# Low splits moved in VectorE's order, and a small fp32 matmul ahead of three units of each FFN

## The reference

```
def hybrid_layer(x, gain, w_in, f_bias, w_branch, w_out):      # first block, twice
    h = rms_norm(x, gain); proj = h @ w_in                     # q, k, v, gates, merge logits
    oa, ob, oc = moba(...), dsa(...), forgetting(...)          # each times silu(gate)
    y = einsum(stack([oa, ob, oc]), w_branch)
    return x + sum(sigmoid(merge_logit) * y) @ w_out
...
x = rms_norm(x, final_gain)
for layer in range(2):                                         # second block
    mod, mod_c = silu(c) @ ada_w[layer] + ada_b[layer], silu(c_ctx) @ ada_w[layer] + ada_b[layer]
    h   = modulate(x,   norm1_g[layer], sh1,  sc1)
    h_c = modulate(ctx, norm1_g[layer], csh1, csc1)
    if layer == 0: y, y_c = even_mixer(h, ...), even_mixer(h_c, ...)     # ends in "@ w_out"
    else:          y = neighbourhood_attention(q, k, v, k_c, v_c, rpb) @ odd_w_o
    x = x + g1 * y
    x = x + g2 * conv_ffn(modulate(x, norm2_g[layer], sh2, sc2), w_up, conv_w, conv_b, w_down)
    if layer == 0: ctx goes the same way as x
return x
```

## Time and profile before

| | us |
|---|---|
| runs, median of three | 1611.9 (1608.91 to 1612.96) |
| the profiled execution | 1592.3 |
| its span, first to last instruction | 1590.5 |
| TensorE busy | 1541.7 |
| VectorE busy | 1039.8 |
| ScalarE busy | 754.3 |
| GpSimd busy | 97.5 |

### The profile page before, as it was taken

The page is one execution under the profiler, slowest core; times in us unless marked ns, Lnnn a source line. Parts: engine busy times, 40 slices in busy tenths (PEclk is TensorE's granted clock), DMA queues, the critical chain, the costliest instruction groups (busy, mean ns, idle before and its releaser), DMA issues.

```text
span 1590.5 us, 31408 instructions
## 1 busy us (share of the span) xinstructions
PE 1541.7 (97%) x13587; PEld 1474.1 (93%) x13587; DVE 1039.8 (65%) x1347; ACT 754.3 (47%) x1132; POOL 97.5 (6%) x79
## 2 busy tenths in 40 slices
PE   6999999999999999999999999999999999989999
PEld 5998999999998999999899999999999996889999
DVE  5878667577877675655457668886445447666675
ACT  5554555455455554554346321333245426655453
POOL 0311000003010000000010000000010102000000
PEclk9999999999999999999999999999999999989999
DMA  8677454566775546522034657754334424255754
GB/s 272 213 239 226 147 182 142 180 222 211 239 238 159 186 148 207 174 80 80 28 107 146 199 178 233 239 186 143 90 116 146 115 80 96 76 148 153 232 170 136
DMA packets 312333, 260.92 MB, mean 164 GB/s; under 512 B 24066, under 2 KB 298498, under 8 KB 312068
## 3 DMA queue, kind: packets, MB, share of 16 engines
q1 hardware_dynamic: 294260, 253.52, 50.2%
q10 hardware_dynamic: 17936, 5.40, 1.6%
HBM read 257.85 MB, written 1.05 MB: 163 GB/s over the span
## 4 chain that ended last, share of the span: by engine, by line
PE 76%; DVE 9%; issue 8%; ACT 6%; DMA 1%; POOL 0%; ACTq 0%; DVEq 0%; SPq 0%; POOLq 0%
PE banks_g L1388 33%; PE banks_g L945 23%; PE banks_g L1118 5%; PE banks_g L935 4%; DVE w_lo L2462 2%; PE banks_g L1260 2%; PE banks_g L968 1%; PE bank_s L1066 1%; ACT w_hi L1761 1%; PE bank_o L1093 1%; PE bank_t L1079 1%; ACT probs L1725 1%; DVE w_lo L2167 1%; ACT w_hi L1565 1%; PE banks_g L927 1%
## 5 line engine op out<-in xcount | busy, mean ns | idle before, releaser
L1388 PE MATMUL banks_g<-h_hi,w_lo 128*128 128x256 f32 x1296 | 360.7, 278 | 3.9 <-DVE w_lo L2462 2.9
L1388 PE MATMUL banks_g<-h_lo,w_hi 128*128 128x256 f32 x1296 | 359.0, 277 | 0.0
L1388 PE MATMUL banks_g<-h_hi,w_hi 128*128 128x256 f32 x1296 | 359.0, 277 | 0.0
L2462 DVE TENSOR_TENSOR w_lo<-raw,w_hi 128x2048 fp32r<-128x2048 f32 (+1 forms) x100 | 207.6, 2076 | 103.3 <-ACT w_hi L1761 103.2
L2167 DVE TENSOR_TENSOR w_lo<-raw,w_hi 128x2048 fp32r<-128x2048 f32 x92 | 212.4, 2311 | 69.4 <-ACT w_hi L1565 68.9
L1388 PEld LDWEIGHTS banks_g<-h_hi,w_lo 128*128 128x128 f32 x1296 | 244.3, 189 | 5.9 <-DVE w_lo L2462 3.3
L1388 PEld LDWEIGHTS banks_g<-h_lo,w_hi 128*128 128x128 f32 x1296 | 244.3, 188 | 0.1
L1388 PEld LDWEIGHTS banks_g<-h_hi,w_hi 128*128 128x128 f32 x1296 | 244.0, 188 | 0.0
L945 PE MATMUL banks_g<-h_hi,w_lo 128*128 128x256 f32 x800 | 225.4, 282 | 0.0
L945 PE MATMUL banks_g<-h_hi,w_hi 128*128 128x256 f32 x800 | 221.8, 277 | 0.0
L945 PE MATMUL banks_g<-h_lo,w_hi 128*128 128x256 f32 x800 | 221.7, 277 | 0.0
(11 more groups left out here) (406 smaller groups left out, 3274.0 us busy)
## 6 DMA issues: line engine op xcount, KB each, us to landing
raw<-w_in SPq DMA_DIRECT2D x76, 1024.0 KB, 5.0
raw<-w_up SPq DMA_DIRECT2D x88, 512.0 KB, 5.1
ada_raw<-ada_w SPq DMA_DIRECT2D x24, 1024.0 KB, 7.0
raw<-w_down SPq DMA_DIRECT2D x32, 704.0 KB, 4.4
raw<-w_branch SPq DMA_DIRECT2D x12, 1024.0 KB, 5.0
ada_raw<-ada_t SPq DMA_DIRECT2D x12, 1024.0 KB, 4.9
late_raw<-ada_t SPq DMA_DIRECT2D x12, 1024.0 KB, 5.0
raw<-qkv SPq DMA_DIRECT2D x12, 1024.0 KB, 4.9
```

Of the source, the lines that this page charges most:

```text
L1388: last = nc.tensor.matmul(to, w[:, c, m0:m0 + P], a[:, c, s_ * SEQ:s_ * SEQ + SEQ], start=(m, s_, c, n) == (0, 0, 0, 0), stop=(m, s_, c, n ...
L2462: nc.vector.tensor_tensor(w_lo[:, u % SLOTS, 0:n], raw[:, u % SLOTS, 0:n], w_hi[:, u % SLOTS, 0:n].bitcast(F32), ALU.subtract).then_inc(dv ...
```

## The change

Five moves in the order of the splits, a new order inside unit eo 0, and six new matmuls.

```diff
@@ layer_order: the context rows' entries 1 to 3, up to three units later @@
-        if 41 <= n <= 44:
-            order.append(("ctx prep", n - 41))
+        order.extend(("ctx prep", m) for m, at in enumerate((41, 44, 44, 45)) if n == at)
@@ end_order, down0 units 14 and 15, before the second block's first unit @@
                 order.append(("ahead", "nq", 0))
+                order.append(("ahead", "nq", 1))
+                chunks("10", 0, 5, KC)
                 part("down0", KC + 6, 1, 6)
-                chunks("10", 0, 5, KC)
-                order.append(("ahead", "nq", 1))
                 part("down0", KC + 7, 1, 7)
@@ end_order, the even mixer's output @@
     for i in range(4):
+        if i == 0:
+            order.append(("ahead", "eo", 2))
         part("eo", i, 0, 2 * i, 2 * i + 1)
-        if i < 2:
-            order.append(("ahead", "eo", i + 2))
+        if i == 1:
+            order.append(("ahead", "eo", 3))
@@ end_order, the attention's output; unit wo 3 no longer splits up1 1 itself @@
         order.append(("unit", "wo", i))
+        if i == 2:
+            order.append(("ahead", "up1", 1))
@@ TensorE, unit eo 0 of the x tokens (of_rows: the three products of chunk c, half m) @@
+                    if (kind, i, j) == ("eo", 0, 0):
+                        for c in (0, 1, 2, 4, 5, 6, 3, 7):
+                            pe.wait_ge(dve_steps, dve_.at(f"a lo{c}" if c < 4 else f"b lo{c - 4}"))
+                            if c == 3:
+                                for c1 in (0, 1, 2, 4, 5, 6):
+                                    of_rows(gb, wh, wl, c1, 1, c1 == 0, False)
+                            of_rows(gb, wh, wl, c, 0, c == 0, False)
+                        for c in (3, 7):
+                            last = of_rows(gb, wh, wl, c, 1, False, c == 7)
@@ TensorE, ahead of the products of units 2, 3 and 4 of each FFN @@
+                            if kind in ("up0", "up1") and j == 0 and 2 <= i <= 4:
+                                nc.tensor.matmul(gb[0:32, 0:HD], ones[:, 0:32], ones[:, 0:HD], start=True, stop=True)
@@ VectorE, end of the first block: both first low splits behind the last output unit @@
-                        if i >= 2:
+                        if layer < DEPTH - 1 and i >= 2:
                             first_low(i - 2)
+                        elif i == 3:
+                            first_low(0)
+                            first_low(1)
```

More of the change, by code:

```diff
@@ L1234, in down_pair, with of_rows @@
                             mm.then_inc(pe_steps, pe_.step(f"job{ks[n]}", f"unit{u0 + n}"))
+            def of_rows(gb, wh, wl, c, m, first, last):
+                for n, (w, a) in enumerate(((wl, f_hi), (wh, f_lo), (wh, f_hi))):
+                    mm = nc.tensor.matmul(gb[:, m * SEQ:m * SEQ + SEQ], w[:, c, m * P:m * P + P], a[:, c, 0:SEQ],
+                                          start=first and m == 0 and n == 0, stop=last and n == 2)
+                return mm
             for what, *arg in END:
@@ L1264, in _ @@
                         continue
+                    if (kind, i, j) == ("eo", 0, 0):
[7 more added lines that the diff above has]
+                            last = of_rows(gb, wh, wl, c, 1, False, c == 7)
+                        last.then_inc(pe_steps, pe_.step(f"job{k}"))
+                        continue
                     for m in range(wide // P):
                         for c in range(kcs):
-                            if (kind, i, j, m) == ("eo", 0, 0, 0):
-                                pe.wait_ge(dve_steps, dve_.at(f"a lo{c}" if c < 4 else f"b lo{c - 4}"))
                             if (kind, i, j) in SUMS_INSIDE and (m, c) == (wide // P - 1, 4):
@@ L1827, in _ @@
                     late = kind == "up0" and i < 2
-                    if u + AHEAD < len(END_UNITS) and not late:
+                    if u + AHEAD < len(END_UNITS) and not late and (kind, i) != ("wo", 3):
                         high(u + AHEAD)
```

## The result

The changed kernel takes 1589.3 us (median of 4 executions, 1586.9 to 1590.4) against 1610.4 us (4 executions, 1605.3 to 1613.0); the ratio is 0.9884, 95% interval 0.9843 to 0.9924. It is faster by 1.2%, and the time lies 3.3 us above the forecast of 1586. Its profiled execution took 1589.1 us, span 1587.3.

A forecast was written before the change was run, and what follows sets the result against it. TensorE was taken as the bound, through matmul spacing and waits. Gains 4.1 + 1.9 + 1.7 + 1.2 less 2.4 for leads make 6.5 us; 1592.3 - 6.5 = 1585.8, taken as 1586, range 1580 to 1592.

The forecast's parts named there:

- A: Both FFNs: leads re-draw the matmul spacing, so slow streams turn fast and fast ones stay; 1586 us, chance 0.50.
- Even mixer's and attention's output projection: Reordered splits shorten TensorE's waits in both output projections: 1.9 us (1.0 to 2.2) and 1.7 us (0 to 3.2).
- Second block's first unit: Queries nq 0 and nq 1: splits placed together remove a TensorE wait and the half clock behind it, 4.1 us.
- End of the first block: Context-row preparation and first low splits moved to shorten two TensorE waits: 1.2 us gained, bounds -1.0 and 3.0.
- The longer chain for the last output unit: End of the first block: chain grows from 7.3 to about 9.7 us, against the 10.9 us of two units.
- Leads: Six small fp32 matmuls before units 2, 3 and 4 of each FFN: 0.4 us each, 2.4 us unhidden cost.
- Sum of the moves: Gains of the moved splits at four places, 4.1, 1.9, 1.7 and 1.2 us, before the leads' cost.
- the base: Three timed runs, 19.6 us above the profiled execution, had both FFNs slow: 4752 matmuls at 4.4 ns, 20.9 us.
- a new draw, not a switch: TensorE's stream: a small fp32 matmul draws the spacing anew, 113.4 or 117.8 ns, rather than switching it.
- Rival B: FFNs: leads do not turn the stream, or the 19.6 us has another cause; only splits count, 1605.4 us, chance 0.34.
- Rival C: Only one FFN is turned, or only one was slow: 1591.5 or 1598.4 us, chance 0.08.
- D: Leads leave the stream slow in FFNs that ran fast: price 20.9 us, 1626 us, chance 0.08.

The follow-up runs named there:

- second trace of before: The kernel before, unmodified, profiled once more in a follow-up run: 1607.6 us.
- set 2: Second batch of follow-up executions, each against the kernel before; the changed kernel, unmodified, ran again in it: 1588.2 us, ratio 0.9897.
- set 3: Third batch of follow-up executions; the changed kernel without the leads of unit 2 took 1588.2 us there, 0.9936 against the kernel before.

## Why the prediction was right, and where not

The forecast (A, 1586 us) and its two halves held: the moved splits take waits off TensorE, and the leads keep the first FFN at the fast spacing. Step by step:

- **Even mixer's and attention's output projection**, forecast 1.9 + 1.7 us: 3.2 us by undoing them. In the stretches of the traces it is 1.9 and 1.9. The wait left at eo 3 is 0.21 us where 0.4 was expected; that for the norm sum is 2.35 in the first trace of the changed kernel and 1.94 in the second, where 1.8 was expected.
- **Second block's first unit**, forecast 4.1 us (2.0 to 4.2): 2.4 us by undoing it, though wait and half clock both went as the text said. In the traces the stretch is 3.9 to 4.2 us shorter in all ten with the new order, so the term was right. That the whole showed only 2.4 us isn't explained; the ranges of the two kernels touch (1590.3 to 1596.0, 1585.0 to 1591.0).
- **End of the first block**, forecast 1.2 us: 1.9 us by undoing it, 2.0 by the stretches. The second wait fell by more than I took: 0.79 us in the first trace of before was the shortest of the four with the old order, the others have 1.53, 2.15 and 2.17. The longer chain for the last output unit, which I had put at nothing, cost 0.69 us at 670.93, in the second trace of the changed kernel 0.28. In the first pair of traces the waits fell by 0.96 and 0.23 us and 0.69 came new, with 10.2 us of half clock in both, and the stretch seemed to gain nothing.
- **Leads**, forecast 0.4 us each: 0.43, so 2.6 us for six where 2.4 were taken.
- **Sum of the moves**, forecast 8.9 us before the leads' cost: 9.5 and 8.6 group against group, 7.5 as the sum of the three undone parts (2.4 + 3.2 + 1.9), 9.9 by the stretches of the traces.

The step that failed is the base: "the three runs had both FFNs at the slow spacing and the profiled one had them at the fast one". The second trace of before shows only the first FFN slow, worth 12.0 us and not 20.9; the second was fast in 13 of 14 traces but for the first few units, and in the one with a single lead in front of unit 2 its last 864 matmuls were slow. The rest of the 19.6 us is the choice of executions: the profiled one lay 3.7 us below the median of its own lower group (1592.3 against 1596.0 over 41 low executions in three sets), and the median of the three runs, 1611.9, lay 3.5 us above that of the upper group (1608.4 over 47). Part of the 3.7 us shows in the traces: the end of the first block ran 1.6 to 3.2 us shorter there than in the three others with its order. That 19.6 came so near to 20.9 was luck. The forecast of 1586 starts from the profiled execution and so from a base that was 3.7 us too low; that is about all that it missed by, and the range of 6 us to each side held it. By the runs the account is 1608.4 (the upper group, in which all four of the first comparison lay) - 12.0 (spacing) - 9.9 (moves, by the stretches; 7.5 by undoing) + 2.6 (leads) = 1589.1, or 1591.5 with 7.5; measured 1589.1.

A second reading did not hold: the prediction calls a small fp32 matmul in the stream "a new draw, not a switch". Behind the wait in front of unit 2 the spacing does differ between two traces of one kernel (fast and slow for the kernel before, slow and fast for the changed one); behind a group of small fp32 matmuls in a running stream it was settled, in each of the four places counted above, by the group and the spacing that came in.

Rival B (leads are pure cost) is refuted by the leads alone, 0.9958 with an interval below 1. The Trainium skill, TensorE: Matmul & The Clock Gate (Back-to-back issue gap), gives one gap for one number of columns. The traces disagree: here the same 2712 matmuls take 307.62 or 319.65 us at full clock. Rival C (one FFN turned) is near the truth as to the size of the slow part. D didn't come: of 76 fp32 leads in a running stream in ten traces, 69 met a fast stream and left it fast, 7 a slow one, of which 6 turned it. Behind the wait in front of unit 2 the stream came out slow in three of eight traces with a lead there, and in three of six without. So the forecast's theory, that fast stays fast and slow is turned by each lead, holds in 75 of 76 cases of a running stream; for the lead behind the wait these traces show no effect.

How much the leads bring depends on how often the first FFN would be slow. For the kernel before that was 4 of 4 executions in the first comparison, then 20 of 29, 14 of 23 and 9 of 32. The ratio of the changed kernel moves with it: 0.9884 in the first comparison, 0.9897 in set 2; in set 3 the kernel with leads in front of units 3 and 4 alone had 0.9936.

Open: what sets the spacing behind a wait; why an fp32 lead keeps a fast stream and an fp32r lead doesn't (two leads of the latter in one trace), where other fp32 groups turn it over; and where all of the 8 us of scatter inside the lower group come from. The traces show parts of it: the first matmul starts up to 2.1 us later in one than in another (the first load), the end of the first block differs by up to 3.2 us between traces of one order, and some short stretches run slow.

## What to carry over

A profile is one execution. Before its time is used as a base, set it against the spread of the timed ones: two groups with nothing between are a state to be found, and count its matmuls per window first. Undo parts one at a time and compare groups with like groups; a pair of spans showed 3.2 us where the moves gave about 9. To price one move, measure its stretch between the same two instructions in every trace at hand: that told 4.0 us from 2.4 where whole times could not. In a TensorE-bound stream of this form a tiny fp32 matmul (0.43 us) can only pay where the stream would run slow and more than some 100 matmuls follow (0.43 us over 4.4 ns, an estimate), and in a running stream rather than behind a wait; two of them did as well as three.

## What was not expected of the hardware

- How long the clock stays at half differs between executions at one place: at the end of the first block the stretches add up to 6.8 us in three of the 14 traces, 10.2 in nine and 13.7 in two. At the output projection they were 10.2 us in all four traces that have its old order, and 6.8 us in six of the ten with the new one.
- One fp32r matmul form has two spacings at full clock, 113.3 and 117.8 ns, and keeps one for up to 2776 matmuls: 12.0 us, or 0.75% of the kernel.
- The spacing can change where the stream is broken. Behind one wait it came out fast in eight traces and slow in six. An fp32 matmul of 32 x 64 in a running stream left it fast in 75 of 76 cases; an fp32r one of the same size turned it once each way.
- Other small fp32 groups in a running stream turn the spacing over, from fast to slow and from slow to fast alike: the eight of `head_sum` in 14 of 14 traces, the four of `head_spread` behind them in 14 of 14, the norm sum in 12 of 12.
- The main split in the kernel's time follows from it: cut at 1603 us, medians of the lower and the upper group of the kernel before are 1596.9 and 1608.5, 1595.1 and 1608.2, 1596.1 and 1608.3 us in the three sets.
